# The small experts' output rows as one plain float32 copy, scattered by plain products

## The reference

```
logits = (xt @ router);  top_v, top_i = top_k(logits, 2);  top_w = softmax(top_v)
gates = sum(one_hot(top_i, 8) * top_w[..., None], axis=1)
for e in range(8):
    out = out + gates[:, e:e+1] * swiglu(xt, w_in[e], w_out[e])   # 1024 -> 2 x 3584 -> 1024
h = layer_norm(ALPHA * h + out)
```

## Time and profile before

| | us |
|---|---|
| runs shown | 1399.9, 1399.89, 1394.12 (median 1399.89) |
| profiled execution | 1394.54 |
| its span | 1392.8 |
| PE busy | 1363.7 (98%) |
| PE weight loads busy | 1155.8 (83%) |
| VectorE busy | 1142.2 (82%) |
| ScalarE busy | 970.3 (70%) |
| chain that ended last, by engine | PE 55%, DVE 38%, issue 4%, ACT 2% |

### The profile page before, as it was taken

How to read it: one execution, slowest core, us unless ns; L and a number is a source line. 1 busy time by engine, 2 the same in 40 slices (tenths; PEclk the granted TensorE clock), 3 DMA queues, 4 the chain that set the end, 5 groups by cost and what they waited for, 6 DMA issues and landing times.

```text
span 1392.8 us, 18184 instructions
## 1 busy us (share of the span) xinstructions
PE 1363.7 (98%) x7168; PEld 1155.8 (83%) x7168; DVE 1142.2 (82%) x825; ACT 970.3 (70%) x830; POOL 68.8 (5%) x65
## 2 busy tenths in 40 slices
PE   9999999999999999999999999999999999999996
PEld 9987789999989888878788878788878788878784
DVE  5455656444475669999999999999999999999997
ACT  5334444333454448888997888997888897888894
POOL 1001301000010003000200000200000000000000
PEclk9999999999999999999999999999999999999998
DMA  9654547555555427999999999999999999999991
GB/s 355 236 167 165 195 153 241 182 181 183 189 188 197 145 98 294 423 421 422 419 418 423 414 412 421 412 418 423 396 421 418 409 419 424 394 423 423 420 418 74
DMA packets 144405, 446.85 MB, mean 321 GB/s; under 512 B 7088, under 2 KB 46000, under 8 KB 129984
## 3 DMA queue, kind: packets, MB, share of 16 engines
q1 hardware_dynamic: 142496, 439.38, 80.8%
q0 software_dynamic: 1824, 6.33, 1.3%
HBM read 444.63 MB, written 1.05 MB: 320 GB/s over the span
## 4 chain that ended last, share of the span: by engine, by line
PE 55%; DVE 38%; issue 4%; ACT 2%; POOL 1%; DMA 0%; DVEq 0%; SPq 0%; ACTq 0%; POOLq 0%
DVE wlo L1066 24%; PE ps L1548 15%; PE ps L1550 15%; PE ps L1549 15%; DVE wlo_more L1066 7%; PE ps L1990 2%; PE ps L1991 2%; DVE gT_lo L1066 1%; DVE act L1435 1%; DVE h L1426 1%; PE ps L1891 1%; PE ps L2030 1%; ACT whi_more L901 1%; PE ps L1593 1%; POOL wlo L673 1%
## 5 line engine op out<-in xcount | busy, mean ns | idle before, releaser
L1066 DVE TENSOR_TENSOR wlo<-raw,whi 128x2048 fp32r<-128x2048 f32 (+1 forms) x214 | 477.9, 2260 | 4.5 <-ACT whi L901 4.3
L901 ACT ACTIVATE whi<-raw 128x2048 fp32r<-128x2048 f32 x208 | 395.6, 1918 | 74.0 <-PE ps L1550 69.9
L435 DVE TENSOR_TENSOR wlo<-raw,whi 128x2048 fp32r<-128x2048 f32 x78 | 179.0, 2295 | 149.8 <-ACT whi L428 149.6
L428 ACT ACTIVATE whi<-raw 128x2048 fp32r<-128x2048 f32 x82 | 156.7, 1911 | 146.9 <-PE ps L1550 143.3
L1548 PE MATMUL ps<-xT_hi,whi 128*128 128x256 f32 x576 | 163.4, 284 | 0.0
L1550 PE MATMUL ps<-xT_hi,wlo 128*128 128x256 f32 x576 | 163.0, 283 | 0.0
L1549 PE MATMUL ps<-xT_lo,whi 128*128 128x256 f32 x576 | 163.0, 283 | 0.0
L1990 PE MATMUL ps<-whi,xg_small 128*128 128x512 f32 x336 | 132.6, 395 | 0.9 <-DVE wlo L1066 0.9
L1548 PE MATMUL ps<-whi,xg_big 128*128 128x512 f32 x336 | 132.2, 393 | 0.2
L1991 PE MATMUL ps<-wlo,xg_small 128*128 128x512 f32 x336 | 131.1, 390 | 0.0
L1550 PE MATMUL ps<-whi,xg_big 128*128 128x512 f32 x336 | 131.0, 390 | 0.0
(11 more groups left out here) (270 smaller groups left out, 2692.4 us busy)
## 6 DMA issues: line engine op xcount, KB each, us to landing
raw<-in_moe_w_in SPq DMA_DIRECT2D x166, 1024.0 KB, 9.1
raw<-in_moe_w_out SPq DMA_DIRECT2D x86, 1024.0 KB, 9.4
more_raw<-in_moe_w_in SPq DMA_DIRECT2D x58, 1024.0 KB, 9.1
more_raw<-in_moe_w_out SPq DMA_DIRECT2D x26, 1024.0 KB, 9.5
raw<-in_ret_w_in SPq DMA_DIRECT2D x23, 1024.0 KB, 7.0
raw<-in_ffn_w_in SPq DMA_DIRECT2D x22, 1024.0 KB, 4.9
raw<-in_ffn_w_out SPq DMA_DIRECT2D x11, 1024.0 KB, 4.9
raw<-in_ret_w_out SPq DMA_DIRECT2D x8, 1024.0 KB, 4.9
```

Source lines behind the costliest of these rows:

```text
L428: nc.scalar.activation(whi[:, u % SPLIT, :], src, ACT.Copy).then_inc(hi_done, 1)
L435: nc.vector.tensor_tensor(wlo[:, u % SPLIT, :], src, whi[:, u % SPLIT, :].bitcast(F32), ALU.subtract).then_inc(lo_done, 1)
L901: nc.scalar.activation(moe_split(n)[0], moe_raw(n), ACT.Copy).then_inc(hi_done, 1)
L1066: return nc.vector.tensor_tensor(dst, src, hi.bitcast(F32), ALU.subtract)
```

## The change

For small jobs ScalarE's copy goes to a float32 buffer y_plain, which lies where y_hi lay; VectorE's subtraction of jobs 1, 3 and 5 is left out; and PE scatters these jobs' rows by one plain float32 product for each half, as `scatter_rows` does for job 7, after a wait on ScalarE's copy instead of one on VectorE's low part. As y_lo_done is now counted by big jobs alone, their wait becomes j + 2. Two float32r products with 512 columns are so replaced by one plain float32 product, twelve times in all.

```diff
--- before.py
+++ after.py
@@ -243,6 +243,7 @@
         xg_big = [place(f"xg_big{i}", [P, KD, 2, P], F32R, at=xT_at + i * 8192)[0] for i in range(2)]
         y_hi = [place(f"y_hi{i}", [P, D], F32R, at=xT_at + i * 8192)[0] for i in range(2)]
         y_lo = [place(f"y_lo{i}", [P, D], F32R, at=xT_at + i * 8192 + 4096)[0] for i in range(2)]
+        y_plain = [place(f"y_plain{i}", [P, D], at=xT_at + i * 8192)[0] for i in range(2)]
         ln_last, _ = place("ln_last", [P, 2, D], at=xT_at)
         whi_more, _ = place("whi_more", [P, UNIT], F32R, at=ln_gb_at)
         xg_again, _ = place("xg_again", [P, KD, 2, P], F32R, at=ln_gb_at)
@@ -1020,7 +1021,7 @@
                     j = Y_AT[n]
                     if j > 0:
                         act.wait_ge(scattered, T * j)
-                    drain_y(U_MOE + n + 1, 4 + 2 * (j % 2), y_hi[j // 2 % 2])
+                    drain_y(U_MOE + n + 1, 4 + 2 * (j % 2), (y_plain if SMALL[j] else y_hi)[j // 2 % 2])
             drain_y(U_AGAIN, 6, y_last)
 
             act.wait_ge(over_ready, 1)
@@ -1497,7 +1498,8 @@
                 big_drains(n)
                 if n - 1 in Y_AT:
                     j = Y_AT[n - 1]
-                    drain_y(j, 4 + 2 * (j % 2), y_hi[j // 2 % 2], y_lo[j // 2 % 2])
+                    if not SMALL[j]:
+                        drain_y(j, 4 + 2 * (j % 2), y_hi[j // 2 % 2], y_lo[j // 2 % 2])
                 if n in ADD_AT:
                     j, t = ADD_AT[n]
                     at = 1 + POSITION[j]
@@ -1923,10 +1925,10 @@
                                      start=False, stop=True)
                 last.then_inc(scattered, 1)
 
-            def scatter_rows(t, half, at):
+            def scatter_rows(t, half, at, rows=y_last):
 
                 return pe.matmul(ps[:, at + half, :], selT[1][:, t * P:(t + 1) * P].bitcast(F32),
-                                 y_last[:, half * BANK:(half + 1) * BANK], start=True, stop=True)
+                                 rows[:, half * BANK:(half + 1) * BANK], start=True, stop=True)
 
             def pieces(b, q):
 
@@ -2070,10 +2072,18 @@
                 if n in SCATTER_AT:
                     j, t = SCATTER_AT[n]
                     pe.wait_ge(selT_ready, j + 1)
-                    pe.wait_ge(y_lo_done, 2 * j + 2)
+                    if SMALL[j]:
+                        pe.wait_ge(y_hi_done, 2 * j + 2)
+                    else:
+                        pe.wait_ge(y_lo_done, j + 2)
                     if t == 1 and j < JOBS - 2:
                         pe.wait_ge(summed, T * j + 1)
-                    scatter(t, selT[j % 2], y_hi[j // 2 % 2], y_lo[j // 2 % 2], scatter_bank(j, t))
+                    if SMALL[j]:
+                        for half in range(2):
+                            last = scatter_rows(t, half, scatter_bank(j, t), y_plain[j // 2 % 2])
+                        last.then_inc(scattered, 1)
+                    else:
+                        scatter(t, selT[j % 2], y_hi[j // 2 % 2], y_lo[j // 2 % 2], scatter_bank(j, t))
                 if n in SEL_AT:
                     j = SEL_AT[n]
                     pe.wait_ge(big_silu, 7 * (j // 2) + 5)
```

## The result

The changed kernel takes 1398.24 us (median of 20 runs, 1397.41 to 1403.7), the kernel before 1397.03 us (20 runs, 1393.76 to 1400.95). The ratio is 1.0027, 95% interval [1.0014, 1.004]: 0.27% slower, 3.8 us, where 4.4 us were forecast. The interval leaves out 1, and the change is inside the 0.5% that the forecast called no change. The profiled execution took 1397.64 us.

A forecast was written before the change was run, and what follows sets the result against it. Limit taken to pass from VectorE to PE at 768, and over ScalarE back to VectorE at 815. Jobs 1 and 3 (3.26 us) plus job 5 (1.17) made 4.4 us, added to 1397.1: 1401.5 us, range 1395.5 to 1406.5.

The forecast's parts named there:

- The price of the plain product: Small jobs' scatters on PE: two records of 0.43 us, 0.86 us a product, so 0.82 us more a scatter.
- rival (b): Plain products' weight loads stand open between float32r products on PE: 9.0 us slower in all, 1406.1 us; chance 0.08.
- The removed subtractions count for nothing: VectorE's saving in jobs 1 and 3, 1.19 us each, goes into its lead over PE: no gain.
- rival (a): VectorE is the limit all the way and PE has slack: 3.6 us gained, 1393.5 us at most; chance 0.07.
- The lower bound of 1.19 us a job: Jobs 1 and 3: gain of up to 1.19 us a job from VectorE's subtractions, were PE not the limit there.
- the zero: Gain of nothing from the removed subtractions in jobs 1 and 3, covered by PE's own work from 768 to 813.
- the waits from 768.5 to 813 us: Around job 1's scatters PE never waits for VectorE; it idles only 0.5 us (own issue) and 0.3 us (ScalarE).
- the terms: Shift of PE's later work by its longer scatters: 1.63 us each for jobs 1 and 3, 1.17 for job 5.
- rival (c): PE's added 1.6 us a job is partly absorbed by margins elsewhere: 0 to 2.5 us, in the middle 1398.3; chance 0.20.
- The third term's other margin: Job 5: 0.46 us between ScalarE's whi and VectorE's subtraction reading it, taken off 1.63 to give 1.17 us.
- PE still runs without a wait on VectorE: Sign of being right: no PE wait on VectorE from PE's start at the scatters' place to the handover.
- VectorE's idle time: Sign of being right: VectorE idles more, by 3.6 us and the longer span together.

The follow-up runs named there:

- e4: The changed kernel with each plain product of jobs 1, 3 and 5 issued twice; ratio 1.0100 to the kernel before.
- e1: The changed kernel with VectorE's six subtractions of jobs 1, 3 and 5 put back, their result unread; ratio 1.0037 to the kernel before.
- e2: The kernel before without the six subtractions of jobs 1, 3 and 5, its second float32r product reading y_hi again; ratio 1.0012 to the kernel before.
- e5: The changed kernel with tile 0's scatter of jobs 1, 3 and 5 one unit earlier; ratio 1.0003 to the kernel before.
- e6: The kernel before with low parts of jobs 1, 3 and 5 subtracted on GpSimd from an extra ScalarE copy; ratio 1.0019 to the kernel before.

## Why the prediction was right, and where it was off

- **The price of the plain product**, on which the sum rests, held: 0.80 and 0.81 us a scatter in the change, 0.864 us a product in e4. The two records with 0.43 us between them, read from job 7 at the end of the kernel, are also its price in a full stream; rival (b) has no support, and the plain loads are 0.187 to 0.192 us and hidden. The Trainium skill's rule on the fast weight load (page "TensorE: Matmul & The Clock Gate", section "Weight-path perf modes") is not borne out as a cost here.
- **The removed subtractions count for nothing once PE is later**: shown by e1. But "nothing" is true only beside the added PE work. Alone they were worth 1.5 us (e2), so rival (a)'s 3.6 us are wrong as well. The lower bound of 1.19 us a job was too generous, and the zero was taken without its condition.
- **The step that failed** is the one on the waits from 768.5 to 813 us: "PE's only idle times are 0.5 us of its own issue and 0.3 us behind a ScalarE result". The 0.5 us were a wait for VectorE's wlo, as the times at 789 show, and e2, in which VectorE's relief alone takes it away. It made the forecast too large by 0.32 us a job in all three places, 0.96 of the 1.07 us missing. With it the terms become 1.3, 1.3 and 0.85; measured 1.31, 1.22 and 0.85. So rival (c) had a share in the truth, a margin met by the shift, at a place that I had ruled out. The third term's other margin, 0.46 us between ScalarE's whi and its reader, was sized right.
- **The signs named ahead**: y_lo has 8 subtractions, the scatter's records step by 0.43 us, ScalarE's waits on PE grow by 1.6 us (7.5 to 9.1 us in that stretch, in e1 and in the changed kernel), and the distances grow by less than forecast. "PE still runs without a wait on VectorE" was true of the changed kernel and not of the one before. VectorE's idle time, span less busy time, grew by 4.7 us (250.6 to 255.3), where 3.6 us and the longer span, 6.6 us, were named.
- **DMA** played no part in what the runs can show: its share in the pair is 1.02 as before, with 414 GB/s, and the shift in the upper group of times is nearly that of the lower (3.34 and 3.63 us), so nothing was hidden there either.
- **The median**: 1401.5 was built on the mean of four times, two in each group. Of the 20 runs of the changed kernel 11 fell in the lower group, and the median lies in it. That the whole time came out 3.3 us under the number forecast says nothing of the mechanism; it is the luck of the groups. The lower group alone moved from 1394.14 to 1397.77, the upper from 1399.94 to 1403.28.

## What to carry to other kernels

Where two engines are both nearly full, ask of the very stretch of the edit which one holds the other: here PE's microseconds behind jobs 1 and 3 counted nearly in full in both directions once its waits were gone, VectorE's only as far as PE had waits to give up. A short idle time labelled "issue" can be a wait for another engine, and then it is a margin that the first delay eats; compare the end of the instruction that could be awaited before calling it the engine's own. Here the load followed 0.20 to 0.21 us behind VectorE's next start each time; the 0.24 us of the plain loads, under the same label, recur every 0.43 us whatever VectorE does. Work that has lost its dependence on a late engine may be moved into a wait that it couldn't use before (e5), and work moved to an idle engine is free only if it does not slow its neighbour (e6).

## What the runs showed of the hardware that I had not expected

**Two groups of times.** The kernels here have two groups of execution times some 5.5 us apart (before: ten runs at 1394.14 and ten at 1399.94 on average); only e4's four and e5's ten runs all fell in the lower one. They part where the experts' stage begins: the gathers of the first pair start at 519.42 us in the kernel before and its products at 523.67, not at about 550 as said ahead of the prediction. The stretch 515 to 530 us of three profiled executions, before, changed and e1 (1403.65 us, of the upper group), columns as in the earlier trace rows:

```profile
515.00:530.00 15.00, 15.00 (x93) 13.91 (x93) 13.49 (x24) 9.87 (x9) 0.00 (x0) 0.89 0.01 2
```

```profile
515.00:530.00 15.00, 14.93 (x101) 13.55 (x102) 14.49 (x29) 11.03 (x10) 0.00 (x0) 1.00 0.01 2
```

```profile
515.00:530.00 15.00, 15.00 (x75) 14.16 (x75) 11.81 (x21) 7.72 (x7) 0.00 (x0) 0.58 0.01 2
```

The granted clock is 0.89, 1.00 and 0.58, and the anchor behind it stands at 551.39, 551.07 and 556.73 us. In e1 PE's products there (start, length):

```profile
514.16 1.85 PE L1875 MATMUL ps<-router,xT 128*128 128x8 f32 x16
...
516.31 1.45 PE L1594 MATMUL ps<-ident 128*128 128x128 f32 x10
...
520.37 0.63 PE L1892 MATMUL ps<-sel,h_hi 128*128 128x128 f32 x2
520.79 0.63 PE L1892 MATMUL ps<-sel,h_lo 128*128 128x128 f32 x2
```

Up to 516 us PE does router products with 8 columns and short fillers; then the gathers run at 0.42 us a pair, the 1.2 GHz level, where the kernel before has 0.22 from 519.88 us on. So the two groups differ by how long TensorE is granted 1.2 instead of 2.4 GHz behind the router, and the anchor by 5.3 to 5.7 us. e2's profiled execution, of the upper group too, has a clock of 0.57 in that stretch and its anchor at 556.53; the seven of the lower group have 0.89 or 1.00 and 550.98 to 551.79. What decides it in a given execution the runs don't say, and no kernel here tried to change it.

**GpSimd beside VectorE.** Eight 128x512 products of two tiles in SBUF took 1.3 us each on GpSimd in the dense stage (L641, median 1297 ns), but the subtractions of e6 3.2 us each beside VectorE's 128x2048 ones, which were slowed with them: 1.6 us on two of them. (Lengths on GpSimd are rough in this profile.) The Trainium skill, page "SBUF — State Buffer", section "SBUF: two separate sides", says that the two engines share one port pair as an exclusive lock, which a VectorE instruction with two SBUF inputs needs too, and that the loser blocks for the whole instruction. The trace agrees in that both engines were slowed while they ran side by side; that it was the port no run here shows. By that rule e6's relief could not be free. My own number for it had left that out, and only the rival named it.
